# A larger share of the gate table on GpSimd, scalar-form subtractions beside it, and a re-ordered start

## The chip, the cores and the metric

One core of one Trainium2 chip runs the whole program. The metric is device microseconds of one execution; lower is better. Engines are named as the profile names them: PE (TensorE), ACT (ScalarE), DVE (VectorE), POOL (GpSimd), SP (SyncE, which here only issues DMAs).

## The reference, cut to what matters

A decoder trunk of two layers, 256 tokens, width 1024, float32. `c_act = silu(c)`, and per layer `mod = c_act @ w_mod[i] + b_mod[i]` gives six vectors of 1024: shift, scale and gate of the mixer, shift, scale and gate of the expert part. Layer 0 mixes with a gated short convolution (`conv_in`, `conv_out`), layer 1 with multi-scale pooling (`pool_in`, `pool_group`, `pool_out`). Then both do this:

```python
h = modulate(rmsnorm(x, norm2_g[i]), sh2, sc2)
# peer_ffn: 8 heads, product keys 128 x 128 = 16384 experts, 16 chosen per head and token
idx  = e1 * N_KEYS + e2                      # chosen experts of a token
gate = softmax(sc)                           # their weights
act  = gelu(sum_d(xc * u_tab[idx]))
out  = sum(gate * act * v_tab[idx])
x = x + g2 * out
```

A final RMS norm gives the output.

## The kernel before, in words

**The expert part is done densely.** For all 16384 experts, as 128 tiles of 128 experts, PE multiplies the `up` tile with all 256 tokens; ACT applies GELU; the result, `acts` (A), has 128 blocks of 128 experts x 256 tokens. It is then multiplied by a gate matrix that is zero but for the chosen experts, and PE multiplies it with the 128 `down` tiles (`down_banks`, L1779). The `down` tiles are taken in two halves of 64 (half 0, then half 1). Float32 products are made of three products of rounded parts: each weight tile is loaded by SP into `raw` (ring of 4), ACT rounds it to `high` (L546), DVE subtracts to get `low` (`rest_of`, called through `slot`, L833), always three tiles ahead of PE; the moving side is split alike into `mov_h` (ACT L752) and `mov_l` (`low_weight`, DVE L1382).

**The gate matrix comes in three ways.** Tokens 0 to 127: POOL adds the gates into a table in device memory with 128 indirect DMAs per layer (`add_gates`, L494), SP fetches it back, and DVE multiplies it in (`weigh_first`, L1239), two tiles of experts at a time. Tokens 128 to 255, first 64 tiles: DVE builds one-hot matrices of 8 tokens, a "set" (`hots`, L1215, L1217, L1221), PE turns each set into a gate block with 24 matmuls (`scatter`, L1729), DVE multiplies it in (`weigh`, L1233), 16 sets. Same tokens, last 64 tiles: the first `LATE_T` = 80 of them again by POOL (`add_late`, L505: per layer `LATE_S` x 8 heads x 2 = 5 x 8 x 2 = 80 indirect DMAs; then `fetch_late`, L517, and on DVE `weigh_late`, L1247), the other 48 tokens by 6 sets, taken in pairs (48 matmuls) among the first `down` tiles of half 0.

**Order on POOL.** All of `add_gates`; then, once SP has fetched the packed lists of indices and gates (`fetched`, L426; that fetch waits until the sets whose space it overwrites have been built, and stands after `up` tile `LATE_UP` in SP's queue), all of `add_late`; then a wait for all of them to land; then `fetch_late`, four buffers.

**Order on DVE in half 0.** For each of the 64 tiles: `slot`, `low_weight`, `weigh_first`, at some tiles `two_sets`, and at the last three tiles `weigh_late` for the first buffers. DVE takes its instructions in order, so a `weigh_late` whose buffer has not landed holds everything behind it, the next `low` and `mov_l` among them.

**The start.** Sixteen blocks of 512 KB of `w_mod` (scale: m = 1, shift: m = 0, k = 0 to 7) are loaded in ten DMAs (`HEAD`, six of them of two blocks), DVE accumulates them (L856, L857), PE sums over the partitions (L1500), ACT adds the shift (L599), and PE starts the convolution's first two tiles (`first_two`, L1571).

Of the kernel before, what the change touches and what calls it, by code (L numbers as in the profile page):

```python
# [34 lines left out]
LATE_T = 80  # L35
LATE_UP = 112
# [31 lines left out]
HEAD = [(1, 0, 1), (1, 1, 1), (1, 2, 2), (1, 4, 2), (1, 6, 2), (0, 0, 2), (0, 2, 2), (0, 4, 2), (0, 6, 1), (0, 7, 1)]  # L68
# [32 lines left out]
def program(nc, small, x_in, k_t, w_mod, conv_in, conv_out, query, up, down, pool_in, pool_group, pool_out,  # L101
# [8 lines left out]
    with ExitStack() as ctx:  # L110
# [146 lines left out]
        macc_done = sem("macc_done")  # L257
        msum_done = sem("msum_done")
# [57 lines left out]
        def _(sp):  # L316
# [19 lines left out]

            for n, (m, k, ks) in enumerate(HEAD):
# [4 lines left out]
                sp.dma_start(mhead[:, m, k:k + ks],  # L342
                             w_mod[0, k * P:(k + ks) * P, m * D:(m + 1) * D].rearrange("(k p) n -> p k n", p=P)
                             ).then_inc(mhead_in[n], 16)
# [194 lines left out]
        def _(act):  # L539
# [36 lines left out]
            def norm(k):  # L576


                if k == 0:
                    act.wait_ge(x_in_s, 16)  # L580
                    for c in range(DC):
                        square(c)
                elif k % 2:
                    act.dma_start(x_spill, flat2(X)).then_inc(spilled, 16)
                act.wait_ge(stat_done, k + 1)
                nc.scalar.activation(sd, gp[:, 0, 0:TC], ACT.Sqrt, bias=eps[:, 0:1],
                                     scale=1.0 / D).then_inc(sd_done, 1)
                if k == 4:
                    return
                if k == 0:  # L590
                    for n in range(AHEAD):
                        arrived(1, n)
                        nc.scalar.activation(flat(high[n]), tile_row(n), ACT.Copy).then_inc(high_ready, 1)
                shift = mod[:, (3 * (k % 2)) * DC:(3 * (k % 2) + 1) * DC]

                act.wait_ge(mod_taken, 4 * (2, 4, 6, 6)[k])
                for c in range(DC):
                    act.wait_ge(xr_done, DC * k + c + 1)
                    nc.scalar.activation(mov_h[:, c], xr[:, c], ACT.Identity,  # L599
                                         bias=shift[:, c:c + 1]).then_inc(mh_done, 1)  # L600

# [219 lines left out]
        def _(dve):  # L821
# [6 lines left out]
            def rest_of(n):  # L828
# [7 lines left out]
            def slot(n):  # L836

                rest_of(n + AHEAD)
# [20 lines left out]
            def head_mod(m):  # L859

                for n, (block_, k0, ks) in enumerate(HEAD):
                    if block_ == m:
                        dve.wait_ge(mhead_in[n], 16)
                        for k in range(k0, k0 + ks):
                            link(add_mod(m, mhead[:, m, k], k, k == 0))
                dve.sem_inc(macc_done, 1)
# [3 lines left out]
            def finish_mod(layer, m0, m1):  # L870

                sums[0] += 1
                dve.wait_ge(msum_done, sums[0])
# [18 lines left out]
            def norm(k, shift_last=None):  # L892
# [3 lines left out]
                if k == 0:  # L896
                    head_mod(1)
# [8 lines left out]
                if k == 0:  # L906
                    head_mod(0)
                    link(nc.vector.memset(vp[:, :, 0:TAPS - 1], 0.0))
                    finish_mod(0, 1, 2)
# [24 lines left out]
                for c in range(DC):  # L934
                    if k == 0 and c == 2:
                        rest_of(0)
                        shift_last()
                    scaled(c)
                if k == 0:
                    rest_of(1)  # L940
                if k == 2:
                    rest_of(AT[1, "pool_in"] + 2)
                if k < 4:
                    for c in range(DC):
                        rest(c)
                if k == 0:
                    rest_of(2)

# [286 lines left out]
            def weigh_first(layer, q):  # L1235
# [30 lines left out]
            for layer in range(LAYERS):  # L1266
                if layer == 0:
                    norm(0, lambda: finish_mod(0, 0, 1))
# [109 lines left out]
                def low_weight(g):  # L1378
                    if g < KEYS:
                        s = g % RING  # L1380
                        dve.wait_ge(wh_ready, g + (layer * KEYS + 1))
                        nc.vector.tensor_tensor(mov_l[:, s], A[:, g * T:(g + 1) * T], mov_h[:, s].bitcast(F32),  # L1382
                                                ALU.subtract).then_inc(wl_ready, 1)
# [8 lines left out]
                for j in range(FIRST_SET, KEYS):  # L1392
# [6 lines left out]
                    slot(n0 + j)  # L1399
# [91 lines left out]
        def _(pe):  # L1491
# [5 lines left out]
            def mod_products(m, c0=0, c1=DC):  # L1497

                for c in range(c0, c1):
                    ins = nc.tensor.matmul(gp[:, 1, m * DC + c:m * DC + c + 1], macc[:, m, c * P:(c + 1) * P],  # L1500
                                           ones[:, 0:1], start=True, stop=True)
                return ins

            def sum_mod(m):

                if sums[0]:

                    pe.wait_ge(mod_taken, 4 * sums[0])
                sums[0] += 1
                mod_products(m).then_inc(msum_done, 1)  # L1510
# [53 lines left out]
            def first_two(layer, name, evac, evac0):  # L1564

                late = name == "conv_in"
                pe.wait_ge(low_ready, AT[layer, name] + (1 if late else 2))
# [5 lines left out]
                for c in range(DC):  # L1573
                    pe.wait_ge(mh_done, moved[0] * DC + c + 1)
                    for s in range(2):
                        one(s, high, mov_h, c, c == 0, False)
                        if s == 0 or not late:
                            one(s, low, mov_h, c, False, False)
                if late:
                    pe.wait_ge(low_ready, AT[layer, name] + 2)  # L1580
                    for c in range(DC):
                        one(1, low, mov_h, c, False, False)
# [72 lines left out]
            for layer in range(LAYERS):  # L1655
                out_act = layer * (16 + KEYS)
                if layer == 0:
                    square_sums(0, 0, DC)
                    pe.wait_ge(macc_done, 1)
                    sum_mod(1)  # L1660
# [242 lines left out]
```

## Time and profile before

| | us |
|---|---|
| three runs | 1806.35, 1812.38, 1812.19 (median 1812.19) |
| the profiled execution's own time | 1807.06 |
| its span, first to last instruction | 1805.4 |
| PE busy | 1765.9 (98% of the span) |
| DVE busy | 1443.1 (80%) |
| POOL busy | 839.8 (47%) |
| mean granted TensorE clock | 0.992 |

The profile's times are from the span's start. PE is busy nearly throughout, so a change counts as far as it shortens PE's work or makes PE wait. Rows of a timeline give start, duration, engine, source line and operation, and in brackets the engine's idle time before and what ended it.

### The profile page before, as it was taken

To read this page: it belongs to the slowest core of one execution; us is meant where nothing else is said; L and a number is where in the kernel's file an instruction comes from. 1 tells how busy PE (TensorE), PEld (TensorE's weight loads), DVE (VectorE), ACT (ScalarE), POOL (GpSimd) and SP (SyncE) were. 2 spreads that over 40 slices of the span, in tenths; PEclk is the share of its full clock that TensorE was granted. 3 is DMA by queue.
4 is the path that set the end of the run, shared out by engine and by line. 5 is a ranking of instruction groups with operands and counts; after the bars stand their busy time and mean duration, and the time that the engine had idled before them with its cause. 6 is when DMAs were issued, how large, how long until landed. Compare 5 with 4: busy or idle time off the path is not lost.

```text
span 1805.4 us, 34572 instructions
## 1 busy us (share of the span) xinstructions
PE 1765.9 (98%) x11751; PEld 1593.7 (88%) x11751; DVE 1443.1 (80%) x2758; ACT 928.3 (51%) x1449; POOL 839.8 (47%) x489
## 2 busy tenths in 40 slices
PE   6999999999999999999998999999999999999998
PEld 6988999999888888888888899999988888888887
DVE  8998789997777966698888778999787796666665
ACT  3345555555555445454555546556555554545453
POOL 1000066777877888510000005677777888841000
PEclk9999999999999999999999999999999999999998
DMA  8998889867766988999945756777777698886662
GB/s 322 325 338 315 273 256 303 252 175 189 175 172 166 249 233 242 295 362 334 325 164 179 265 164 164 186 179 183 186 175 179 164 244 234 241 262 205 209 207 85
DMA packets 191697, 414.23 MB, mean 229 GB/s; under 512 B 77696, under 2 KB 95488, under 8 KB 190976
## 3 DMA queue, kind: packets, MB, share of 16 engines
q1 hardware_dynamic: 126768, 405.36, 66.7%
q0 software_dynamic: 62976, 5.49, 8.6%
q10 hardware_dynamic: 1872, 2.39, 0.4%
q8 instruction: 40, 0.66, 0.1%
q14 instruction: 41, 0.34, 0.1%
HBM read 387.60 MB, written 25.54 MB: 229 GB/s over the span
## 4 chain that ended last, share of the span: by engine, by line
PE 93%; DVE 5%; issue 1%; DMA 1%; ACT 1%; SPq 0%; DVEq 0%; ACTq 0%
PE acc L1779 38%; PE ps L1597 31%; PE ps L1614 7%; PE acc L1614 5%; PE ps L1617 4%; PE acc L1617 2%; PE gp L1729 2%; DVE acts L857 2%; PE ps L1571 1%; DVE low L833 1%; PE gp L1718 1%; DMA acts<-w_mod 1%; DVE acts L924 0%; PE gp L1533 0%; DVE mov L956 0%
## 5 line engine op out<-in xcount | busy, mean ns | idle before, releaser
L833 DVE TENSOR_TENSOR low<-raw,high 128x1024 fp32r<-128x1024 f32 x596 | 724.0, 1217 | 276.1 <-ACT high L546 273.5
L546 ACT ACTIVATE high<-raw 128x1024 fp32r<-128x1024 f32 (+1 forms) x593 | 624.7, 1054 | 375.3 <-PE acc L1779 300.8
L494 POOL DMA_INDIRECT table<-added x256 | 466.3, 1821 | 585.4 <-DVE added L1080 452.7
L1779 PE MATMUL acc<-high,mov 128*128 128x512 f32 x2048 | 633.9, 390 | 2.7 <-DVE mov L1382 2.7
L1597 PE MATMUL ps<-mov,high 128*128 128x256 f32 x3280 | 594.0, 284 | 7.2 <-issue 2.7
L1597 PEld LDWEIGHTS ps<-mov,high 128*128 128x128 f32 x3280 | 511.0, 192 | 9.1 <-issue 6.1
L1597 PE MATMUL ps<-mov,low 128*128 128x256 f32 x1640 | 463.9, 283 | 0.0
L1779 PEld LDWEIGHTS acc<-high,mov 128*128 128x128 f32 x2048 | 384.4, 188 | 84.4 <-DVE mov L1382 2.7
L1779 PE MATMUL acc<-low,mov 128*128 128x512 f32 x1024 | 398.4, 389 | 0.0
L1597 PEld LDWEIGHTS ps<-mov,low 128*128 128x128 f32 x1640 | 314.6, 192 | 0.0
L1779 PEld LDWEIGHTS acc<-low,mov 128*128 128x128 f32 x1024 | 192.2, 188 | 39.6
L505 POOL DMA_INDIRECT late<-gate x96 | 198.4, 2066 | 35.7 <-issue 28.7
L517 POOL DMA_DIRECT2D mov<-late x64 | 34.7, 544 | 270.2 <-DVE acts L1247 262.2
L691 ACT ACTIVATE acts<-ps 128x256 f32<-128x256 f32 x160 | 61.2, 382 | 191.8 <-PE ps L1597 191.6
L1614 PE MATMUL ps<-mov,high 128*128 128x512 f32 x592 | 149.3, 394 | 0.5 <-DVE low L833 0.5
L505 POOL DMA_INDIRECT late<-idx x64 | 135.6, 2119 | 19.5 <-issue 19.5
L1614 PEld LDWEIGHTS ps<-mov,high 128*128 128x128 f32 x592 | 106.3, 189 | 20.2 <-issue 0.9
L857 DVE SCALAR_TENSOR_TENSOR acts<-acts,cact 128x1024 f32<-128x1024 f32 x86 | 109.9, 1278 | 3.3 <-DMA acts<-w_mod 2.9
L752 ACT ACTIVATE mov<-acts 128x256 fp32r (+1 forms) x256 | 101.9, 400 | 20.0 <-DVE acts L1239 20.0
L1382 DVE TENSOR_TENSOR mov<-acts,mov 128x256 fp32r<-128x256 f32 x256 | 106.5, 418 | 2.3 <-ACT mov L752 2.3
L1614 PE MATMUL acc<-mov,high 128*128 128x512 f32 x384 | 97.0, 394 | 0.0
L1617 PEld LDWEIGHTS ps<-mov,low 128*128 128x128 f32 x592 | 80.8, 190 | 5.8
(156 smaller groups left out, 1410.8 us busy)
## 6 DMA issues: line engine op xcount, KB each, us to landing
raw<-up SPq DMA_DIRECT2D x256, 512.0 KB
raw<-down SPq DMA_DIRECT2D x256, 512.0 KB
acts<-w_mod SPq DMA_DIRECT2D x84, 512.0 KB, 5.8
raw<-query SPq DMA_DIRECT2D x32, 512.0 KB
table<-hot SPq DMA_DIRECT2D x32, 512.0 KB, 6.7
raw<-conv_in SPq DMA_DIRECT2D x24, 512.0 KB
mov<-table SPq DMA_DIRECT2D x96, 128.0 KB, 4.3
acts<-w_mod SPq DMA_DIRECT2D x6, 1024.0 KB, 14.9
```

The source lines that it names most:

```text
L494: nc.gpsimd.indirect_dma_start(table[layer], bass.IndirectOffsetOnAxis(ap=DEST[:, col:col + 1], axis=0), GT0[:, col:col + 1], None, comput ...
L505: nc.gpsimd.indirect_dma_start(table2[layer], bass.IndirectOffsetOnAxis(ap=LATE_AT[m][:, col:col + 1], axis=0), LATE_GATE[m][:, col:col + ...
L546: nc.scalar.activation(taken_of(n, flat(high[s])), taken_of(n, tile_row(s)), ACT.Copy).then_inc(high_ready, 1)
L691: nc.scalar.activation(A[:, bass.ds(i * (RING * T) + (first + s) * T, T)], ps[:, s % 2, 0:T], ACT.Gelu).then_inc(evac_act, 1)
L752: nc.scalar.activation(mov_h[:, s], A[:, bass.ds(g * T, T)] if not isinstance(g, int) else A[:, g * T:(g + 1) * T], ACT.Copy).then_inc(wh_ ...
L833: nc.vector.tensor_tensor(taken_of(n, flat(low[n % RING])), taken_of(n, tile_row(n % RING)), w, ALU.subtract).then_inc(low_ready, 1)
L857: return nc.vector.scalar_tensor_tensor(macc[:, m], tile, c, macc[:, m], ALU.mult, ALU.add)
L1382: nc.vector.tensor_tensor(mov_l[:, s], A[:, g * T:(g + 1) * T], mov_h[:, s].bitcast(F32), ALU.subtract).then_inc(wl_ready, 1)
L1597: ins = nc.tensor.matmul(dst, w[s][:, c], m[:, mv], start=(first and n == 0), stop=(last and n == 2), skip_group_check=skip)
L1614: nc.tensor.matmul(b, high[s][:, c], flat(mov[:, c]), start=(c == 0), stop=(c == DC - 1), skip_group_check=True)
L1617: ins = nc.tensor.matmul(b[:, 0:T], low[s][:, c], mov_h[:, c], start=False, stop=(c == DC - 1), skip_group_check=True)
L1779: ins = nc.tensor.matmul(acc[:, b, :], w[:, s, tok], flat(v[s])[:, cols], start=(opening and n == 0), stop=(closing and n == 2), skip_grou ...
```

## The change

`LATE_T` goes from 80 to 96: `LATE_S` becomes 6, so POOL gets 6 x 8 x 2 = 96 indirect DMAs of `add_late` per layer instead of 80, and four sets remain instead of six. `LATE_UP` goes from 112 to 116. In the `up` tiles from the 81st on and in half 0 of `down`, DVE's subtractions (`slot`, in half 0 also `low_weight`) and the products of `weigh_first` are written as `scalar_tensor_tensor` with a factor 1.0 in place of `tensor_tensor`. At the start every block of `w_mod` has a DMA of its own, DVE does four shift blocks before it finishes the scale and four behind it (the last in two halves), the shift is summed in two halves, and PE takes the high parts of the first two tiles before their low parts, with one filler matmul (`keep_warm`) per chunk.

```diff
-LATE_T = 80
-LATE_UP = 112
+LATE_T = 96
+LATE_UP = 116
-HEAD = [(1, 0, 1), (1, 1, 1), (1, 2, 2), (1, 4, 2), (1, 6, 2), (0, 0, 2), (0, 2, 2), (0, 4, 2), (0, 6, 1), (0, 7, 1)]
+HEAD = [(m, k) for m in (1, 0) for k in range(DC)]
...
+            def two(out, a, b, op, beside_pool=False):
+
+                if beside_pool:
+                    return nc.vector.scalar_tensor_tensor(out, a, 1.0, b, ALU.mult, op)
+                return nc.vector.tensor_tensor(out, a, b, op)
...
-                    nc.vector.tensor_tensor(taken_of(n, flat(low[n % RING])), taken_of(n, tile_row(n % RING)),
-                                            w, ALU.subtract).then_inc(low_ready, 1)
+                    two(taken_of(n, flat(low[n % RING])), taken_of(n, tile_row(n % RING)), w, ALU.subtract,
+                        beside_pool).then_inc(low_ready, 1)
...
+            def finish_shift(c0, c1):
+
+                dve.wait_ge(shift_half, c0 // (DC // 2) + 1)
+                nc.vector.tensor_tensor(mod[:, c0:c1], acc[:, c0 // (DC // 2), c0:c1],
+                                        sm[:, C_BM + c0:C_BM + c1], ALU.add).then_inc(mod_taken, 2)
...
                 if k == 0:
+                    for n in range(4, DC - 1):
+                        link(head_block(0, n))
+                    for h in range(2):
+                        head_block(0, DC - 1, h * D // 2, (h + 1) * D // 2).then_inc(macc_done, 1)
+                    scaled(0)
+                    scaled(1)
+                    finish_shift(0, DC // 2)
+                    scaled(2)
+                    scaled(3)
+                    finish_shift(DC // 2, DC)
+                    sums[0] += 1
+                    scaled(4)
+                    scaled(5)
+                    rest_of(0)
+                    scaled(6)
+                    scaled(7)
                     rest_of(1)
...
-                nc.vector.tensor_tensor(a, a, wt[q % WRING].rearrange("p (g t) -> p g t", t=P),
-                                        ALU.mult).then_inc(weighed, 1)
+                two(a, a, wt[q % WRING].rearrange("p (g t) -> p g t", t=P), ALU.mult, beside_pool
+                    ).then_inc(weighed, 1)
...
-                    slot(n0 + j)
+                    slot(n0 + j, True)
                     fold(side(j - FIRST_SET), j * T).then_inc(folded, 1)
...
-                    slot(n0 + j)
+                    slot(n0 + j, True)
                     if j + AHEAD < HALF:
-                        low_weight(j + AHEAD)
+                        low_weight(j + AHEAD, True)
                     if j < 7:
                         if j % 2 == 0:
-                            weigh_first(layer, j // 2 + 2)
+                            weigh_first(layer, j // 2 + 2, True)
                     else:
-                        weigh_first(layer, j - 1)
+                        weigh_first(layer, j - 1, True)
...
-                    keep_warm(80)
-                    pe.wait_ge(macc_done, 2)
-                    sum_mod(0)
-                    keep_warm(20)
+                    keep_warm(76)
+                    for h in range(2):
+                        pe.wait_ge(macc_done, 2 + h)
+                        sum_shift(h * DC // 2, (h + 1) * DC // 2)
+                    sums[0] += 1
+                    keep_warm(6)
```

## Rows read from the trace of the kernel before

**Rows 1.** The page's chain of waits, shares of the span by line.

```profile
PE acc L1779 38%; PE ps L1597 31%; PE ps L1614 7%; PE acc L1614 5%; PE ps L1617 4%; PE acc L1617 2%; PE gp L1729 2%; DVE acts L857 2%; PE ps L1571 1%; DVE low L833 1%; PE gp L1718 1%; DMA acts<-w_mod 1%; DVE acts L924 0%; PE gp L1533 0%; DVE mov L956 0%
```

**Rows 2.** The chain of waits in order of time: start us, us, what.

```profile
440.07 1.47 PE gp L1729 x48
...
458.38 1.47 PE gp L1729 x48
```

**Rows 3.** POOL's timeline, layer 0, from `add_late` on.

```profile
551.83 2.54 POOL L505 DMA_INDIRECT late<-gate  x1 [4.44 <-DMA table<-added]
...
740.29 2.41 POOL L505 DMA_INDIRECT late<-idx  x1 [0.30 <-issue]
746.77 2.26 POOL L517 DMA_DIRECT2D mov<-late  x4 [4.07 <-DMA late<-idx]
```

**Rows 4.** DVE's timeline, layer 0: the first `weigh_late`.

```profile
751.06 0.32 DVE L1247 TENSOR_TENSOR acts<-acts,mov 128x160 f32<-128x160 f32 x1 [0.94 <-DMA mov<-late]
```

**Rows 5.** The same places of layer 1, POOL's timeline and then DVE's.

```profile
1403.68 2.06 POOL L505 DMA_INDIRECT late<-gate  x1 [2.60 <-DMA table<-added]
...
1592.51 2.43 POOL L505 DMA_INDIRECT late<-idx  x1 [0.30 <-issue]
1598.84 2.26 POOL L517 DMA_DIRECT2D mov<-late  x4 [3.90 <-DMA late<-idx]
...
1610.14 0.32 DVE L1247 TENSOR_TENSOR acts<-acts,mov 128x160 f32<-128x160 f32 x1
```

**Rows 6.** DVE's timeline, then POOL's, in the same microseconds of half 0.

```profile
644.86 1.23 DVE L833 TENSOR_TENSOR low<-raw,high 128x1024 fp32r<-128x1024 f32 x1 [0.82 <-ACT high L546]
646.00 0.42 DVE L1382 TENSOR_TENSOR mov<-acts,mov 128x256 fp32r<-128x256 f32 x1
...
645.09 2.41 POOL L505 DMA_INDIRECT late<-gate  x1 [0.30 <-issue]
```

**Rows 7.** POOL's timeline at another phase against DVE, and DVE's beside it.

```profile
601.51 1.55 POOL L505 DMA_INDIRECT late<-gate  x1 [0.30 <-issue]
603.36 1.55 POOL L505 DMA_INDIRECT late<-gate  x1 [0.30 <-issue]
...
599.71 0.42 DVE L1239 TENSOR_TENSOR acts<-acts,mov 128x256 f32<-128x256 f32 x1
...
603.37 0.46 DVE L1239 TENSOR_TENSOR acts<-acts,mov 128x256 f32<-128x256 f32 x1
```

**Rows 8.** POOL's and DVE's timeline: a scalar-form instruction, in layer 0 and layer 1.

```profile
434.36 1.55 POOL L494 DMA_INDIRECT table<-added  x1 [0.30 <-issue]
...
434.36 0.32 DVE L1194 SCALAR_TENSOR_TENSOR acts<-acts 80x128 f32<-80x128 f32 x1
...
1294.74 0.28 DVE L1194 SCALAR_TENSOR_TENSOR acts<-acts 80x128 f32<-80x128 f32 x1
```

**Rows 9.** Groups by line, shapes kept apart: count, busy us, mean ns, idle before.

```profile
L833 DVE TENSOR_TENSOR low<-raw,high 128x1024 fp32r<-128x1024 f32 x592 | 721.5, 1221 | 276.1 <-ACT high L546 273.5 <-DVE acts L1197 0.2
...
L857 DVE SCALAR_TENSOR_TENSOR acts<-acts,cact 128x1024 f32<-128x1024 f32 x86 | 109.9, 1278 | 3.3 <-DMA acts<-w_mod 2.9
L1382 DVE TENSOR_TENSOR mov<-acts,mov 128x256 fp32r<-128x256 f32 x256 | 106.5, 418 | 2.3 <-ACT mov L752 2.3
...
L930 DVE SCALAR_TENSOR_TENSOR mov<-acts,mod,mov 128x256 fp32r<-128x256 f32 x32 | 13.0, 478 | 0.0
```

**Rows 10.** SP's own queue: the fetch of the packed lists.

```profile
508.29 1.28 SPq L426 DMA_DIRECT2D gate<-shelf  x3
```

**Rows 11.** Busy time by stretch (PE, PEld, DVE, ACT, POOL), granted clock, DMA share, GB/s.

```profile
132.00:139.00 7.00, 4.63 (x36) 4.14 (x34) 6.97 (x10) 2.46 (x5) 0.00 (x0) 1.00 1.00 352
139.00:146.00 7.00, 6.17 (x39) 5.69 (x40) 4.88 (x17) 2.33 (x6) 0.00 (x0) 0.51 0.71 277
```

**Rows 12.** The chain of waits at the start: start us, us, what.

```profile
2.88 9.88 DMA acts<-w_mod
...
46.17 43.44 PE ps L1597 x360
```

More of the change, by code:

```diff
@@ L589, in norm, with first_tile @@
                     return
+                def first_tile(n):
+                    arrived(1, n)
+                    nc.scalar.activation(flat(high[n]), tile_row(n), ACT.Copy).then_inc(high_ready, 1)
                 if k == 0:
-                    for n in range(AHEAD):
-                        arrived(1, n)
-                        nc.scalar.activation(flat(high[n]), tile_row(n), ACT.Copy).then_inc(high_ready, 1)
+                    for n in range(2):
+                        first_tile(n)
                 shift = mod[:, (3 * (k % 2)) * DC:(3 * (k % 2) + 1) * DC]
-                act.wait_ge(mod_taken, 4 * (2, 4, 6, 6)[k])
+                act.wait_ge(mod_taken, 6 if k == 0 else 4 * (2, 4, 6, 6)[k])
                 for c in range(DC):
+                    if k == 0 and c == DC // 2:
+                        act.wait_ge(mod_taken, 8)
                     act.wait_ge(xr_done, DC * k + c + 1)
@@ L906, in norm @@
                 if k == 0:
-                    head_mod(0)
-                    link(nc.vector.memset(vp[:, :, 0:TAPS - 1], 0.0))
+                    for n in range(4):
+                        link(head_block(0, n))
                     finish_mod(0, 1, 2)
@@ L932, in rest @@
                                                    ALU.subtract).then_inc(ml_done, 1)
[L934 to L938, printed above, removed]
-                if k == 0:
+                if k == 0:
+                    for n in range(4, DC - 1):
+                        link(head_block(0, n))
+                    for h in range(2):
[12 more added lines that the diff above has]
+                    scaled(7)
                     rest_of(1)
-                if k == 2:
-                    rest_of(AT[1, "pool_in"] + 2)
-                if k < 4:
+                    dve.wait_ge(mod_taken, 8)
                     for c in range(DC):
                         rest(c)
-                if k == 0:
+                    link(nc.vector.memset(vp[:, :, 0:TAPS - 1], 0.0))
                     rest_of(2)
+                else:
+                    for c in range(DC):
+                        scaled(c)
+                    if k == 2:
+                        rest_of(AT[1, "pool_in"] + 2)
+                    if k < 4:
+                        for c in range(DC):
+                            rest(c)
             moved = [0]
@@ L1381, in low_weight @@
                         dve.wait_ge(wh_ready, g + (layer * KEYS + 1))
[L1382 to L1383 removed]
+                        two(mov_l[:, s], A[:, g * T:(g + 1) * T], mov_h[:, s].bitcast(F32), ALU.subtract,
+                            beside_pool).then_inc(wl_ready, 1)
                 n0 = AT[layer, "up"]
@@ L1571, in one @@
                     return nc.tensor.matmul(ps[:, s, 0:T], w[s][:, c], m[:, c], start=first, stop=last)
-                for c in range(DC):
-                    pe.wait_ge(mh_done, moved[0] * DC + c + 1)
+                if late:
+                    pe.wait_ge(high_ready, 2)
+                    for c in range(DC):
+                        pe.wait_ge(mh_done, moved[0] * DC + c + 1)
+                        for s in range(2):
+                            one(s, high, mov_h, c, c == 0, False)
+                        keep_warm(1)
                     for s in range(2):
-                        one(s, high, mov_h, c, c == 0, False)
-                        if s == 0 or not late:
+                        pe.wait_ge(low_ready, s + 1)
+                        for c in range(DC):
                             one(s, low, mov_h, c, False, False)
-                if late:
+                else:
                     pe.wait_ge(low_ready, AT[layer, name] + 2)
                     for c in range(DC):
-                        one(1, low, mov_h, c, False, False)
+                        pe.wait_ge(mh_done, moved[0] * DC + c + 1)
+                        for s in range(2):
+                            one(s, high, mov_h, c, c == 0, False)
+                            one(s, low, mov_h, c, False, False)
                 lag = DC // 2
```

61 lines of the change are left out of this document (32 added, 29 removed).

## The prediction

> **What bounds the kernel now.** The page's chain of waits is read first, since it says whose work the time is made of: by line it is PE's products and nearly nothing else, with 2% in the one-hot products of L1729 [rows 1]. The one place where a neighbour of PE is nearly late shows in two timelines laid side by side, POOL's and DVE's around tile 61 of half 0. In layer 0 the last `add_late` starts at 740.29 and takes 2.41, so it ends at 742.70; 4.07 later all have landed and the first `fetch_late` is issued at 746.77 [rows 3]. DVE starts the first `weigh_late` at 751.06 after 0.94 us idle for just this buffer [rows 4]. So POOL's chain in layer 0 has no slack at all: it is 0.94 us late. In layer 1 the same step is at 1598.84 and DVE comes at 1610.14 without waiting; with the 4.29 us from issue to use that layer 0 shows (751.06 - 746.77) the slack there is 1610.14 - 1598.84 - 4.29 = 7.0 us [rows 3 to 5]. The change puts 16 more DMAs in front of this point. Whether POOL can take them is the question; all the rest is small.
>
> **What POOL waits for.** The timelines of DVE and POOL over the same microseconds show what one `add_late` costs. The short ones take 1.55 and with 0.30 of issue follow each other by 1.85 [rows 7]. In the steady part of half 0 each takes 2.41 + 0.30 = 2.71, about the 2.72 us of a `down` tile. There POOL starts at 645.09, DVE's L833 has run since 644.86 and gives way to L1382 at 646.00, and POOL ends at 645.09 + 2.41 = 647.50, which is 1.50 after that [rows 6]. So POOL stands still until the `tensor_tensor` with two inputs in SBUF is over, and the next one meets the next tile's L833 in the same way. The reverse is seen too: where POOL and a DVE instruction start together (603.36 and 603.37), POOL is not delayed and DVE's L1239 takes 0.46 in place of 0.42 [rows 7].
>
> **The change, part by part.**
>
> *Fewer sets.* Two sets fewer per layer are one pair of 48 matmuls, 1.47 us on PE's chain with no gap around it [rows 2]. Two layers: -2.94. DVE is rid of one `two_sets` per layer, which hides behind PE.
>
> *Sixteen more indirect DMAs per layer.* Half 0 cannot end before they have landed. They start at 551.83 in layer 0 [rows 3]. The fetch of the packed lists may hold them back: it was at 508.29 [rows 10], and now waits for set 11 in place of set 9, six `up` tiles on, 458.38 - 440.07 = 18.3 us [rows 2], so about 527 plus its landing; the table's own DMAs still end later. With `LATE_UP` at 116, SP stands at this wait with tile 116 and all behind it in its queue; that load comes about one tile and a half late, and a load is issued some seven tiles ahead of PE by the code's waits, so I cost it at nothing; if the cover is gone, it costs about one tile, 3 us.
>
> *The scalar form.* On DVE it costs 1278 - 1221 = 57 ns for a low part and 478 - 418 = 60 ns for each 256-wide product [rows 9], in half 0 57 + 2 x 60 = 0.18 us per tile. That lies in the 0.82 us that DVE idles before each L833 for ACT [rows 6]. With that cover gone it would be 61 x 2 x 0.18 = 22 us. What it does to POOL the trace does not show on a long instruction. Bounds: at best POOL is never held, and the pitch is 1.85; at worst it is held as before, 2.71. The nearest row is the one scalar-form instruction that starts with a POOL DMA, L1194 in layer 0, both at 434.36: it takes 0.32, where the same instruction alone in layer 1 takes 0.28 [rows 8]. That is the same 0.04 that L1239 loses in the same position [rows 7]. The scalar form thus asks for what POOL has, as `tensor_tensor` does. It still reads two tensors in SBUF. I take the worst case, the full hold. The row has one instance, and shows DVE waiting for POOL and not the reverse, which is why the other end keeps a large chance.
>
> The Trainium skill ("SBUF — State Buffer", section "Who interferes with whom") says that a Vector instruction with two SBUF inputs contends with a GpSimd instruction that reads SBUF, and that the first to issue holds the shared pair for its whole length. By that rule the two forms are alike and the sum is the one made below; the rows on `tensor_tensor` agree (1.50 after the end of L833), for the scalar form no row decides.
>
> *The sum with the hold, layer 0.* 16 x 2.71 = 43.4. The third pair of sets is gone, and behind a pair DVE is so busy that POOL slips into the 1.85 pitch; losing some three such DMAs costs 3 x 0.86 = 2.6, an estimate. If DVE ran on, `add_late` would end at 742.70 - 1.47 + 43.4 + 2.6 = 787.2. DVE comes to the first `weigh_late` at 751.06 - 0.94 - 1.47 = 748.65 and stops. From then POOL is free: (787.2 - 748.65) / 2.71 = 14.2 DMAs are left, at 1.85 they take 26.3, to 774.9. Then 4.07 until they have landed and 4.29 until the buffer is there: 783.3. DVE stands for 34.6 in place of 0.94. Behind this `weigh_late` in DVE's order are the next `mov_l` and `low` parts, and PE has about a tile in hand, as now: PE loses 33.7.
>
> *Layer 1.* The last `add_late` ends at 1592.51 + 2.43 = 1594.94 now; with the same additions at 1639.5. DVE stops at 1610.14 - 1.47 = 1608.7; 11.4 DMAs are left, 21.0 us, to 1629.7; then 3.90 and 4.29: 1637.9. PE loses 29.
>
> *The clock.* Where PE had been idle for 2.4 of 7 us, the granted clock of the next 7 us was 0.51 [rows 11], the lower level, 1.2 GHz. After each long stall I add half of 7 us, 3.5: together 7.
>
> *The start.* DVE waits at first for a DMA of two blocks, which lasts 9.88 in the chain [rows 12]. Single blocks let it begin when the first half has landed, about 1.3 us earlier, the length of one block's L857 [rows 9], since DVE then went from block to block without idling for data. Of this, part is given back: the low parts of tiles 0 and 1 stand behind more `scaled` steps, and the last shift block in two halves costs one more instruction's fixed time. PE's unbroken run now begins at 46.17 [rows 12] and depends on the third low part. Bounds: -1.3, and +1.2 if one low part comes late; I take -0.6.
>
> Sum: -2.94 + 33.7 + 29 + 7 - 0.6 = +66. Against the profiled execution's own 1807.06 that is 1873. Its time is 5 us under the median of the three runs, 1812.19, and 0.7 over the lowest, so a median may come 5 higher; I leave the prediction at 1873.
>
> **The rivals.**
>
> *POOL is freed by the scalar form.* All 96 at 1.85 are 178 us: from 551.83 to 729.4, landed at 733.5, fifteen microseconds ahead of DVE. Then nothing waits and most of the 0.94 us is won back too, 0.7: 1807.06 - 2.94 - 0.6 - 0.7 = 1802.8. This ends on the other side, not slower. For it: the form is another instruction with its own pace (57 ns more), and the hold is only shown for `tensor_tensor`. Against: the 0.04 of L1194. The point from which it decides is a mean pitch of (748.65 - 4.07 - 4.29 - 551.83) / 96 = 1.96 us in layer 0, and (1608.7 - 3.90 - 4.29 - 1403.68) / 96 = 2.05 in layer 1 [rows 5]. By this rival and by a median drawn low a gain over 0.5% is possible, hardly more.
>
> *Partly freed.* Only some are held, and the mean pitch is 2.3: `add_late` ends in layer 0 at 551.83 + 96 x 2.3 = 772.6 if DVE runs on, 24 us behind 748.65. Of these, ten DMAs go at 1.85: 767 and 8.4, so 27 us lost; in layer 1 at 1403.68 + 221 = 1624.5, 7 DMAs left, 13 us and 8.2, 21 us lost. With the clock about 1807 + 27 + 21 + 7 - 4 = 1858. At a pitch near 2.05 the loss is under 10 and the time near 1815.
>
> *The scalar form makes DVE the bound.* The 22 us above. Against it: 0.82 idle in each tile, and 0.18 asked; it would need a burst of sets that DVE no longer catches up with, and there are fewer of these now.
>
> **How the numbers follow.** A difference under 0.5%, 9 us, can't be told from none here: the three runs alone spread over 6. Full hold 0.48 (slower). Freed 0.40, of which 0.29 within 0.5% and 0.11 faster, since 4 us of real gain and the spread must add up. Partly freed 0.09, DVE or the start as a new bound 0.03, slower both, but for 0.02 of them within 0.5%. That is slower 0.58, same 0.31, faster 0.11. The likeliest case has its own range of 1855 to 1888: POOL's lateness off by four DMAs either way in both layers, and the clock's 7 in or out. The range for 8 in 10 must reach over the freed case, down to 1799.
>
> **What would show it.** In the profile after: L1729 has 960 matmuls, and 192 rows of L505. In half 0, past the second pair of sets, the rows of L505 last 2.4 to 2.5 if the hold is there, 1.55 if not; this decides all. If it is there, DVE L1247 waits for the DMA of `late` by about 35 and 29 us and PE L1779 for DVE L1382, and the granted clock falls behind it. If not, the first L517 is issued near 733. The unbroken run of PE at the start should begin near 45.6. The prediction is wrong if the low-part rows in scalar form lie over POOL rows that last 1.55.

## Result, and the profile after

| | before | after |
|---|---|---|
| median of the runs, us | 1811.65 (4 runs, 1806.35 to 1812.38) | 1867.18 (4 runs, 1860.57 to 1868.80) |
| ratio after/before | | 1.029, 95% interval 1.0254 to 1.0326 |
| profiled span, us | 1805.4 | 1866.1 |
| mean granted clock | 0.992 | 0.974 |

The kernel is 2.9% slower. 1873 was forecast, with 1855 to 1888 as the likeliest case's own range.

The page's chain of waits, by engine and by line (L1641 and L1825 are PE's products, before L1597 and L1779):

```profile
PE 54%; POOL 29%; issue 6%; DVE 6%; DMA 4%; ACT 1%; SPq 1%; DVEq 0%; POOLq 0%; ACTq 0%
PE ps L1641 22%; POOL late L505 21%; PE acc L1825 19%; POOL table L494 8%; PE ps L1658 4%; PE ps L1661 2%; PE acc L1658 2%; PE ps L1607 2%; DVE low L839 2%; DMA table<-added 1%; DMA raw<-conv_in 1%; PE acc L1661 1%; PE gp L1764 1%; SPq L343 1%; DMA raw<-up 1%
```

Where it was nearly all PE [rows 1], 29% of the span in this chain is now POOL's, 21% in L505 (`add_late`) and 8% in L494 (`add_gates`). That does not mean that POOL's DMAs cost 21% of the time: the chain crosses over to POOL at the two stalls and then follows POOL back. The cost stands in the view of the waits (total, times, longest):

```profile
DVE acts L1284 <- DMA mov<-late: 64.8, 2, 35.1
PE acc L1825 <- DVE mov L839: 63.9, 4, 33.9
```

DVE waits twice, once in each layer, for the buffer of `late`; PE waits for DVE's `mov_l` behind it. Before, the four waits of PE for it summed to 2.7. POOL's timeline in layer 0, to be laid beside [rows 3] and [rows 6]:

```profile
551.92 2.13 POOL L505 DMA_INDIRECT late<-gate  x1 [4.06 <-DMA table<-added]
...
645.93 2.42 POOL L505 DMA_INDIRECT late<-gate  x1 [0.30 <-issue]
...
746.63 2.42 POOL L505 DMA_INDIRECT late<-gate  x1 [0.30 <-issue]
749.35 1.54 POOL L505 DMA_INDIRECT late<-idx  x1 [0.30 <-issue]
751.20 1.55 POOL L505 DMA_INDIRECT late<-idx  x1 [0.30 <-issue]
...
777.10 1.55 POOL L505 DMA_INDIRECT late<-idx  x1 [0.30 <-issue]
780.70 2.25 POOL L517 DMA_DIRECT2D mov<-late  x4 [2.05 <-DMA late<-idx]
```

And DVE's timeline beside it:

```profile
645.71 1.23 DVE L838 SCALAR_TENSOR_TENSOR low<-raw,high 128x1024 fp32r<-128x1024 f32 x1 [0.83 <-ACT high L546]
646.85 0.42 DVE L838 SCALAR_TENSOR_TENSOR mov<-acts,mov 128x256 fp32r<-128x256 f32 x1
...
747.55 0.42 DVE L838 SCALAR_TENSOR_TENSOR acts<-acts,added 128x256 f32<-128x256 f32 x1
783.04 0.36 DVE L1284 TENSOR_TENSOR acts<-acts,mov 128x192 f32<-128x192 f32 x1 [35.07 <-DMA mov<-late]
...
1671.55 0.36 DVE L1284 TENSOR_TENSOR acts<-acts,mov 128x192 f32<-128x192 f32 x1 [29.75 <-DMA mov<-late]
```

Three things are to be read out of the two. First, the low part is now in the scalar form (L838) and the POOL row over it still lasts 2.42. It ends at 645.93 + 2.42 = 648.35, which is 1.50 after L838 hands over at 646.85, the same 1.50 as behind `tensor_tensor` [rows 6]. Second, POOL's rows turn short, 1.54 or 1.55, in the moment in which DVE stands still: from 749.35 to 777.10 there are 1 + 27.75 / 1.85 = 16 of them. Third, with the last of them and 2.05 of landing the fetch comes at 780.70, and DVE goes on 2.34 later.

### The profile page after: what moved, and what is told of

Same layout as the page of the kernel before. It is cut to its first block, busy times and chain, and to the rows that moved or that the text cites. A ratio compares the mean times of both kernels' runs of the same rounds, so it can differ in the third digit from the quotient of the medians.

```text
span 1866.1 us, 34373 instructions
## 1 busy us (share of the span) xinstructions
PE 1766.0 (95%) x11645; PEld 1593.7 (85%) x11645; DVE 1434.0 (77%) x2744; ACT 928.1 (50%) x1449; POOL 908.9 (49%) x521
## 4 chain that ended last, share of the span: by engine, by line
PE 54%; POOL 29%; issue 6%; DVE 6%; DMA 4%; ACT 1%; SPq 1%; DVEq 0%; POOLq 0%; ACTq 0%
PE ps L1641 22%; POOL late L505 21%; PE acc L1825 19%; POOL table L494 8%; PE ps L1658 4%; PE ps L1661 2%; PE acc L1658 2%; PE ps L1607 2%; DVE low L839 2%; DMA table<-added 1%; DMA raw<-conv_in 1%; PE acc L1661 1%; PE gp L1764 1%; SPq L343 1%; DMA raw<-up 1%
## 5 line engine op out<-in xcount | busy, mean ns | idle before, releaser
L494 POOL DMA_INDIRECT table<-added x256 | 469.9, 1835 | 581.4 <-DVE added L1117 448.5
L1825 PE MATMUL acc<-high,mov 128*128 128x512 f32 x2048 | 636.0, 391 | 63.9 <-DVE mov L839 63.9
L1641 PE MATMUL ps<-mov,high 128*128 128x256 f32 x3280 | 595.1, 284 | 6.2 <-issue 2.7
L839 DVE TENSOR_TENSOR low<-raw,high 128x1024 fp32r<-128x1024 f32 x372 | 450.0, 1214 | 164.7 <-ACT high L546 162.9
L1641 PEld LDWEIGHTS ps<-mov,high 128*128 128x128 f32 x3280 | 512.4, 192 | 7.8 <-issue 6.3
L1825 PEld LDWEIGHTS acc<-high,mov 128*128 128x128 f32 x2048 | 386.4, 189 | 145.6 <-DVE mov L839 63.3
L1641 PE MATMUL ps<-mov,low 128*128 128x256 f32 x1640 | 464.6, 283 | 0.0
L1825 PE MATMUL acc<-low,mov 128*128 128x512 f32 x1024 | 399.9, 391 | 0.0
L838 DVE SCALAR_TENSOR_TENSOR low<-raw,high 128x1024 fp32r<-128x1024 f32 x224 | 274.0, 1223 | 122.9 <-ACT high L546 120.4
L1641 PEld LDWEIGHTS ps<-mov,low 128*128 128x128 f32 x1640 | 315.4, 192 | 0.0
L505 POOL DMA_INDIRECT late<-gate x128 | 267.0, 2086 | 45.9 <-issue 38.4
L1825 PEld LDWEIGHTS acc<-low,mov 128*128 128x128 f32 x1024 | 193.4, 189 | 40.0
L517 POOL DMA_DIRECT2D mov<-late x64 | 34.6, 542 | 256.9 <-DVE acts L1284 230.2
L505 POOL DMA_INDIRECT late<-idx x64 | 132.6, 2071 | 19.5 <-issue 19.5
L870 DVE SCALAR_TENSOR_TENSOR acts<-acts,cact 128x1024 f32<-128x1024 f32 x72 | 91.9, 1277 | 0.0
```

The source lines that it names most:

```text
L494: nc.gpsimd.indirect_dma_start(table[layer], bass.IndirectOffsetOnAxis(ap=DEST[:, col:col + 1], axis=0), GT0[:, col:col + 1], None, comput ...
L505: nc.gpsimd.indirect_dma_start(table2[layer], bass.IndirectOffsetOnAxis(ap=LATE_AT[m][:, col:col + 1], axis=0), LATE_GATE[m][:, col:col + ...
L838: return nc.vector.scalar_tensor_tensor(out, a, 1.0, b, ALU.mult, op)
L839: return nc.vector.tensor_tensor(out, a, b, op)
L870: return nc.vector.scalar_tensor_tensor(macc[:, m], tile, c, macc[:, m], ALU.mult, ALU.add)
L1641: ins = nc.tensor.matmul(dst, w[s][:, c], m[:, mv], start=(first and n == 0), stop=(last and n == 2), skip_group_check=skip)
```

## The experiments

In the expectations A is the theory of the prediction: POOL stands through an instruction of DVE that reads two tensors in SBUF, in either form, and sixteen DMAs held in this way are the loss. Ratios are to the kernel before, run beside each kernel on the same chip. The first four kernels take the change apart.

**The tokens alone** (the kernel before with two constants changed):

```diff
-LATE_T = 80
-LATE_UP = 112
+LATE_T = 96
+LATE_UP = 116
```

> The kernel before with 96 tokens in place of 80 and nothing else of the change. Theory A (every long two-input DVE instruction holds POOL, whatever its form; the scalar form does nothing): the same loss as with the whole change, DVE waits near 35 and 30 us at the first weigh_late of each layer, rows of L505 in half 0 at 2.41, time 1867 plus the 0.9 that the new start gives, about 1868. Rival B (the scalar form does relieve POOL in part, so the change hid some of the damage): longer waits than 35 and 30, time above 1875.

Measured: 1871.19 us (1869.76 to 1873.93), ratio 1.034, interval 1.0299 to 1.0381. The waits are those of the whole change, with `tensor_tensor` throughout:

```profile
DVE acts L1247 <- DMA mov<-late: 66.7, 2, 36.9
PE acc L1779 <- DVE mov L1382: 65.8, 4, 35.7
```

The two constants make the whole loss. Rival B, which asked for more than 1875, falls. One row of L505 lasts 7.74 here (from 591.93), which theory A doesn't foresee; it comes back below.

**The scalar form alone** (`slot`, `low_weight` and `weigh_first` as in the change, 80 tokens, the old start; an excerpt of the edit):

```diff
-                    slot(n0 + j)
+                    slot(n0 + j, True)
...
-                        low_weight(j + AHEAD)
+                        low_weight(j + AHEAD, True)
```

> The kernel before, 80 tokens, with the scalar form alone. Theory A: rows of L505 in half 0 stay at 2.41 and the time within 1 us of before (1807 in a profile), since the immediate scalar costs 4 ns on a low part and nothing on the 256-wide products. Rival B: a shorter mean of L505 and no wait of 0.94 us for the late buffer, about 1 us faster.

Measured: 1812.03 (1804.50 to 1819.57, 12 runs), ratio 1.001, interval 0.9986 to 1.0034. The 96 instances of L505 that carry gates (of 160; shortest, median and longest in ns):

```profile
L505 POOL DMA_INDIRECT late<-gate x96: 1546/2402/7736, 545.0 to 1582.9; - x96
```

The median is 2402 ns, as with `tensor_tensor`; the longest, 7.7 us, is again a single row of its kind. The scalar form frees nothing and costs nothing that can be measured. The rival "POOL is freed" falls on this.

**The start alone** (the change with 80 tokens and `LATE_UP` 112, and without the scalar form):

```diff
-                if beside_pool:
-                    return nc.vector.scalar_tensor_tensor(out, a, 1.0, b, ALU.mult, op)
                 return nc.vector.tensor_tensor(out, a, b, op)
```

> The change with 80 tokens and without the scalar form: the new start alone. The profile after shows the end of the convolution stage 0.86 us earlier (first fall of the granted clock at 138.25 in place of 139.11). Expected 0.9 us faster, not measurable in the times; in the profile a span near 1804.5. Rival: the start's gain is lost later in a stage that waits for DVE, span as before.

Measured: 1808.71 (1803.72 to 1818.39, 12 runs), ratio 0.9979, interval 0.9954 to 1.0004. A gain of the start is not told from none. In the profiled execution (span 1810.6) DVE waited once 6.8 us for the buffer of `late`: one row of L505, at 591.27, lasted 7.74, which is 5.3 more than a held one. So here too POOL is at the edge. Behind the convolution PE's first wait for DVE ends at 139.20 here and at 139.72 in the kernel before, 0.52 earlier (0.37 with the whole change, see below), not the 0.86 that the expectation takes from the fall of the clock.

**The change without its sixteen DMAs** (the four sets stay away; the gates of the last sixteen of the 96 tokens are left out of POOL's table, which stays zero there):

```diff
                 for n in range(LATE_S * HEADS):
+                    if n % LATE_S == LATE_S - 1:
+                        continue
                     for k in range(LATE_K):
                         add_late(layer, n, k)
...
-                for n in range(LATE_S):
+                for n in range(LATE_S - 1):
```

> The changed kernel, but POOL leaves out the sixth part of add_late (16 indirect DMAs per layer), so a sixth of the late gates is missing from the output; the rest is as in the change, two sets fewer and the new start too. Theory A: both waits of DVE for the late buffer vanish or stay under 1 us, no clock loss, and the gains stand alone: 1807.1 - 2.9 - 0.9 = 1803. Rival C (the loss is from the other parts of the change: the larger fetches, the later fetch of the lists, LATE_UP): a wait remains and the time stays above 1815.

Measured: 1814.11 (1801.75 to 1827.65, 12 runs), ratio 1.0009, interval 0.9979 to 1.0039. The loss against the kernel before is gone, so it hangs on the number of DMAs. But the median is 11 us above the expected 1803, and the wait did not vanish. By the time alone rival C, which asked for more than 1815, falls only just; it is the view of the waits that says where the 11 us are:

```profile
DVE acts L1286 <- DMA mov<-late: 14.9, 2, 13.9
```

POOL is late even with 80, by 13.9 in layer 0 and 1.0 in layer 1. From the first `add_late` to the end of the last it takes 203.7 in layer 0 (545.04 to 748.69), where the kernel before took 190.9. Two things make this up. With only two pairs of sets left in half 0, fewer of the 80 DMAs are short (22 under 1.9, where 30 were). And one row, at 591.17, lasts 7.74. The spread of 26 us fits a wait that differs from run to run; no low run was profiled.

**Shorter instructions on DVE.** If POOL waits for the end of the instruction that runs, shorter ones should give it 1.85 or near. The low parts are written in two instructions of 512 columns, or four of 256, where the change had the scalar form, with all 96 tokens:

```diff
-                    return nc.vector.scalar_tensor_tensor(out, a, 1.0, b, ALU.mult, op)
...
+                    pieces = 2 if beside_pool else 1
...
+                    for i in range(pieces):
+                        q = slice(i * width, (i + 1) * width)
+                        ins = nc.vector.tensor_tensor(to[:, q], of[:, q], w[:, q], ALU.subtract)
+                    ins.then_inc(low_ready, 1)
```

> The change (96 tokens, new start) with plain tensor_tensor, and each low part from the 81st up tile on and in half 0 done as two instructions of 512 columns. Theory A (POOL stands until the two-input DVE instruction that is running has ended): shorter instructions hold it shorter. By the rows (one half hands over after 0.60 us, POOL needs 1.81 from there to its next start, a tile is 2.72) three of four DMAs meet no or a short remainder and the mean pitch in the steady part falls from 2.72 to 2.04. 96 DMAs then end near 749 in layer 0; DVE waits some 6 us there and about 0 in layer 1: 1806 to 1812. Rival D (POOL gets in only when DVE idles, or it is DVE's total load that counts): the pitch stays 2.72 or grows with the 0.06 us more of DVE work per tile, waits 35 and 30, 1867 or more.

Measured: 1802.52 (1800.34 to 1808.89, 12 runs), ratio 0.9956, interval 0.9939 to 0.9972. The loss is won back, and the kernel is 0.44% faster than before, with 96 tokens. POOL in the steady part of half 0:

```profile
641.76 2.03 POOL L505 DMA_INDIRECT late<-gate  x1 [0.30 <-issue]
644.10 1.82 POOL L505 DMA_INDIRECT late<-gate  x1 [0.30 <-issue]
646.22 1.55 POOL L505 DMA_INDIRECT late<-gate  x1 [0.30 <-issue]
...
649.94 2.03 POOL L505 DMA_INDIRECT late<-gate  x1 [0.30 <-issue]
```

Four DMAs (the line left out is the fourth, at 648.07) in 649.94 - 641.76 = 8.18 us, which is three tiles of 2.72; before it was one in each tile. No wait was left in layer 0, where 6 us were expected, and 7.1 us in layer 1, where none was. Single rows of L505 lasted 7.0 and 7.9 us. Like the rows of 7.74 above they have no place in theory A.

> The same in four instructions of 256 columns, each handing over after 0.335 us. Theory A: mean pitch 1.94, late DMAs end near 740, no wait in either layer, 1803. Rival D: as above and worse, DVE has 0.2 us more work per tile. Rival E (fixed cost of the smaller DVE instructions takes over): POOL is in time but PE waits for low parts behind each pair of sets, time above 1806.

Measured (`pieces = 4`): 1833.19 (1830.92 to 1836.52, 6 runs), ratio 1.0128, interval 1.0102 to 1.0153. Worse than halves by 31 us, and 1803 was missed. The steady part is as expected, four DMAs from 642.19 to 650.02, 1.96 each; the time is lost in a few rows behind the first pair of sets. POOL:

```profile
586.34 6.07 POOL L505 DMA_INDIRECT late<-idx  x1 [0.31 <-issue]
592.71 18.26 POOL L505 DMA_INDIRECT late<-idx  x1 [0.30 <-issue]
611.27 1.54 POOL L505 DMA_INDIRECT late<-idx  x1 [0.30 <-issue]
```

DVE at the end of the 18.26:

```profile
608.80 0.41 DVE L837 TENSOR_TENSOR mov<-acts,mov 128x256 fp32r<-128x256 f32 x1
609.14 0.41 DVE L837 TENSOR_TENSOR acts<-acts,mov 128x256 f32<-128x256 f32 x1
609.47 1.27 DVE L1273 TENSOR_TENSOR acts<-acts,gp 128x512 f32<-128x512 f32 x2
```

DVE has fallen behind with the sets and runs without a gap, one instruction with two SBUF inputs after the other. POOL passes many of their ends without getting in. It ends at 592.71 + 18.26 = 610.97, and 1.50 before that, at 609.47, DVE begins L1273, whose second input, `gp`, is in PSUM. The row of 6.07 ends in the same way, 1.50 after an L1273 that begins at 590.91. So it isn't enough that an instruction ends. But it isn't always such an instruction that lets POOL in either: layer 1's row of 16.26 (from 1467.77) ends 1.51 after 1482.52, where one two-input instruction hands over to the next and DVE is not idle:

```profile
1482.18 0.41 DVE L837 TENSOR_TENSOR acts<-acts,added 128x256 f32<-128x256 f32 x1
1482.52 1.42 DVE L849 TENSOR_TENSOR low<-raw,high 128x256 fp32r<-128x256 f32 x4
```

The expectations of the door below say of both long rows that an input in PSUM ended them; that holds for the one of 18.26 only.

**Less slack needed, and fewer tokens.** Two kernels ask about the 7.1 us left in halves. The first puts the first three `weigh_late` behind the last tile of half 0:

```diff
-                    if j >= HALF - 3:
-                        weigh_late(layer, j - (HALF - 3))
-                for g in range(AHEAD):
-                    low_weight(HALF + g)
+                weigh_late(layer, 0)
+                low_weight(HALF)
+                low_weight(HALF + 1)
+                weigh_late(layer, 1)
+                low_weight(HALF + 2)
+                weigh_late(layer, 2)
```

> low_in_halves with the first three weigh_late moved from the last three tiles of half 0 to behind its last tile. Theory A: DVE asks for the late buffer some 5 us later, so the 6 us of waiting in layer 0 are nearly covered: 1803 to 1806, at the price of at most about 1 us per layer where PE waits for the first mov_l of half 1.

Measured: 1804.39 (1802.45 to 1809.72, 12 runs), ratio 0.9967, interval 0.9951 to 0.9983. The wait for `late` (in layer 1 again) fell from 7.1 to 3.0, but PE's waits for `mov_l` only from 8.3 to 7.3 in all, since the later place adds 0.6 in layer 0. In the time nothing is gained.

The second has halves with 80 tokens:

```diff
-LATE_T = 96
-LATE_UP = 116
+LATE_T = 80
+LATE_UP = 112
```

> low_in_halves with 80 tokens. Theory A: POOL's chain gets 20 to 25 us of slack in place of none, so the late buffer is never waited for, and if the executions of the kernel before above 1807 come from this wait, the spread of times shrinks too: 1805 to 1807 in all runs. Rival F (the spread has another origin): no wait in the profile, but times still spread from 1804 to 1820.

Measured: 1805.32 (1804.11 to 1808.05, 12 runs), ratio 0.9974, interval 0.9959 to 0.999. The fetch goes out at 707.36, 39 us earlier than in the kernel before and with more slack than the 20 to 25 us expected, nothing waits, and the runs lie within 4 us where the start alone and the form alone spread over 15. That the spread comes from the wait for `late` is supported by this, not shown run by run.

**A door for POOL.** The theory formed on quarters (G in the expectations): in an unbroken train of two-input instructions POOL can miss any number of ends, and one instruction with no such input lets it in. So one `memset` of one column was put on DVE in each tile of half 0, behind `weigh_first`:

```diff
+                    if len(doors) >= DC:
+                        need(doors[-DC])
+                    doors.append(did(nc.vector.memset(ctmp[:, j % DC:j % DC + 1], 0.0)))
```

> low_in_quarters with one memset of one column on DVE per tile of half 0, behind weigh_first: 62 ns that read no tensor. In low_in_quarters one L505 lasted 18.26 us (592.71 on) and one of layer 1 16.3 us, both while DVE ran two-input instructions back to back; POOL went on where a product with an input in PSUM began. Theory G (between two-input instructions that follow without a gap POOL may fail to get in, and any instruction that reads at most one SBUF tensor lets it in): no L505 longer than about 3.5 us in half 0, the late DMAs end some 20 us earlier than 752.5, no wait for the late buffer, 1803. Rival H (it is DVE's lack of idle time, a full queue, that shuts POOL out): the long rows remain, and with 0.06 us more of DVE work per tile the time is 1833 or more.

Measured: 1803.93 (1803.20 to 1814.73, 12 runs), ratio 0.9985, interval 0.9967 to 1.0004, against 1.0128 without the `memset`. In the same stretch, behind the first pair of sets, POOL's rows are

```profile
587.97 1.72 POOL L505 DMA_INDIRECT late<-idx  x1 [0.30 <-issue]
...
591.85 2.20 POOL L505 DMA_INDIRECT late<-idx  x1 [0.30 <-issue]
...
596.20 1.70 POOL L505 DMA_INDIRECT late<-gate  x1 [0.30 <-issue]
598.21 1.73 POOL L505 DMA_INDIRECT late<-gate  x1 [0.30 <-issue]
```

and the door itself, on DVE, with the rows that the text below names, is

```profile
592.55 0.41 DVE L1255 TENSOR_TENSOR hot<-sm,idx 128x512 bf16<-128x512 bf16 x1
...
596.42 0.41 DVE L849 TENSOR_TENSOR low<-raw,high 128x256 fp32r<-128x256 f32 x1
596.43 0.06 DVE L1471 MEMSET ctmp<- 128x1 f32 x1
...
598.12 0.06 DVE L1471 MEMSET ctmp<- 128x1 f32 x1
598.44 1.08 DVE L849 TENSOR_TENSOR low<-raw,high 128x256 fp32r<-128x256 f32 x3
```

An instruction of 0.06 us takes away rows of 18.26 and 16.26: the longest row of L505 in half 0 is now 2.20, in either layer (rows of up to 4.53 stand before it, in the `up` stage, where there is no `memset`). Rival H falls. That the `memset` itself is what lets POOL in, as theory G has it, these rows do not show. The DMA of 596.20 ends 1.47 after the first `memset`, but one two-input instruction hands over to the next in the same moment. The DMA of 598.21 ends at 599.94, 1.82 after the second `memset` and 1.50 after an ordinary hand-over at 598.44. And the DMA of 591.85 got in at 592.55, also at an ordinary hand-over, 3 us after the last `memset`. The edit also brings a semaphore wait and shifts DVE by a little in each tile; an instruction as short with two inputs in SBUF, in the same place, was not tried.

> The same memset in low_in_halves, whose longest L505 were 7.0 us in layer 0 and 7.9 in layer 1, in the same place. Theory G: none above 3.5 us, the wait of 7.1 us in the profile of low_in_halves gone, median 1800 to 1802 with a narrower spread than 1800 to 1809. Rival H: unchanged, 1802.5 with the same spread.

Measured (the same lines in halves): 1801.84 (1798.99 to 1806.32, 12 runs), ratio 0.9956, interval 0.9936 to 0.9976, span 1800.0. No wait for `late` is left, and the longest row of L505 in half 0 is 2.07, where halves alone had 7.0 and 7.9. POOL's last rows in layer 0:

```profile
728.90 1.81 POOL L505 DMA_INDIRECT late<-idx  x1 [0.30 <-DMA late<-idx]
734.96 2.25 POOL L517 DMA_DIRECT2D mov<-late  x4 [4.26 <-DMA late<-idx]
```

DVE takes that buffer at 746.53, 11.6 us after the issue. By the ratio it is no better than halves alone, 0.9956 for both; these two are the best versions, 0.44% under the kernel before.

## Why the prediction was right, and where its terms were off

**What POOL waits for.** Right, and it carried the forecast. The scalar form holds POOL as `tensor_tensor` does: 2.42 against 2.41, and 1.50 after the hand-over. The form alone has the ratio 1.001, and the sixteen DMAs with their sets 1.034. The nearest row, the 0.04 that L1194 lost beside a POOL DMA [rows 8], pointed the right way on one instance.

**The sum.** DVE's stalls were forecast as 34.6 and 29.2 (1637.9 - 1608.7), and measured 35.07 and 29.75. PE's waits rose from 2.7 to 63.9, 61.2 more, where 62.7 were in the sum. Two terms inside were off and cancelled. The drain was taken as 4.07 and 3.90; it was 2.05 and, in layer 1, 2.22. The way from issue to use was taken as 4.29 from the kernel before, and was 2.34 and 2.31. In layer 0 that is 4.0 too much. Against it sixteen short DMAs were left when DVE stood, not 14.2: 1.8 more at 1.85, 3.3 us (in layer 1 thirteen, not 11.4). The term behind this is the short rows lost with the third pair of sets: three were estimated, and of the 30 rows under 1.9 in layer 0 only 23 were left outside the stall, seven fewer; in layer 1 22 of 29. So the close hit on the stalls, 34.6 against 35.07, is in part luck. The fetch of the lists and `LATE_UP` were costed at nothing, rightly: the lists are fetched at 526.30 (527 was forecast), and `add_late` starts at 551.92, where it was 551.83.

**The clock.** The windows of after, with PE's, PEld's, DVE's, ACT's and POOL's busy time and then the granted clock:

```profile
745.00:752.00 7.00, 7.00 (x32) 5.79 (x32) 2.14 (x4) 3.18 (x3) 6.08 (x4) 1.00 0.92 264
...
759.00:766.00 7.00, 0.00 (x0) 0.00 (x0) 0.00 (x0) 0.00 (x0) 5.79 (x4) 0.50 0.49 99
787.00:794.00 7.00, 6.74 (x23) 5.42 (x24) 4.72 (x9) 1.37 (x2) 1.08 (x2) 0.75 0.67 214
794.00:801.00 7.00, 7.00 (x33) 5.79 (x32) 7.00 (x10) 3.75 (x6) 0.54 (x1) 1.00 0.81 287
...
1674.00:1681.00 7.00, 5.22 (x12) 4.14 (x13) 4.47 (x10) 1.44 (x3) 1.61 (x3) 0.50 0.84 253
1681.00:1688.00 7.00, 7.00 (x31) 5.76 (x30) 3.44 (x6) 3.87 (x6) 0.27 (x1) 0.98 0.36 108
```

The clock falls to 0.50, the level of 1.2 GHz, while PE stands, and comes back some 3 us after PE goes on at 787.26; in layer 1 it stays low through the 5.22 us that PE works up to 1681. The loss is 0.25 x 6.7 = 1.7 us in the first window and half of 5.22, 2.6, in the other: together 4.3 where 7 were in the sum. A term of the right kind, mis-sized.

**The scalar form's own cost.** The groups of after, by form:

```profile
L839 DVE TENSOR_TENSOR low<-raw,high 128x1024 fp32r<-128x1024 f32 x368 | 447.4, 1219 | 164.7 <-ACT high L546 162.9
L838 DVE SCALAR_TENSOR_TENSOR low<-raw,high 128x1024 fp32r<-128x1024 f32 x224 | 274.0, 1223 | 122.9 <-ACT high L546 120.4 <-issue 2.3
L839 DVE TENSOR_TENSOR mov<-acts,mov 128x256 fp32r<-128x256 f32 x134 | 55.5, 418 | 2.3 <-ACT mov L759 2.3
L838 DVE SCALAR_TENSOR_TENSOR mov<-acts,mov 128x256 fp32r<-128x256 f32 x122 | 51.1, 418 | 0.0
L870 DVE SCALAR_TENSOR_TENSOR acts<-acts,cact 128x1024 f32<-128x1024 f32 x72 | 91.9, 1277 | 0.0
```

57 ns were predicted for a low part and 60 for a 256-wide product; they cost 4 and 0. The rows from which the price was taken [rows 9] have a scalar that is read from a column of a tensor (L870 here, still 1277); with the constant 1.0 the form costs next to nothing. No run changed the scalar alone, so that it makes the difference is a reading. It lay in idle time, so the time did not notice. The rival in which DVE becomes the bound rested on this price, and falls with it.

**The sets and the start.** PE has 960 matmuls of the one-hot products, as forecast, -2.94. The start gains less than the -0.6 that was taken: behind the convolution PE's first wait for DVE ends at 139.35, where it ended at 139.72, 0.37 earlier. DVE begins its unbroken run of six blocks early:

```profile
11.44 7.89 DVE L878 SCALAR_TENSOR_TENSOR acts<-acts,cact 128x1024 f32<-128x1024 f32 x6 [2.37 <-DMA acts<-w_mod]
```

PE's unbroken run starts at 43.21 in place of 46.17 [rows 12], where 45.6 was forecast. But most of this isn't kept. The clock that PE was granted from 32 to 39 is 0.55, where it was 1.00, and the end of the convolution hangs on DVE's blocks, which are themselves only 0.36 earlier (L870 at 136.74, L857 at 137.10 before). In all: -2.94 + 61.2 + 4.3 - 0.4 = 62.2, and the spans differ by 1866.1 - 1805.4 = 60.7; 1.5 stay unexplained.

**The rivals.** "POOL is freed" and "partly freed" both fell with the form alone. The point at which the case turns was put at a mean pitch of 1.96 us in layer 0 and 2.05 in layer 1. Layer 1 bears it out: halves come to 2.12 there (1398.32 to 1602.16), and 96 x 0.07 is the 7 us of the wait. In layer 0 they come to 2.08 and don't wait, because `add_late` starts at 537.9 in this trace, 14 us earlier than the 551.83 of the forecast. With the door nothing waits.

**What stays open.** In the steady part POOL gets in when one two-input instruction hands over to the next (the 1.50 behind L833 and L838), and in the train behind the sets it may not for 18 us. What decides between the two is not shown. The position against DVE's instructions does not, as far as the traces resolve it. Here are the same two places in after and in the start alone:

```profile
591.17 0.68 DVE L1254 TENSOR_TENSOR hot<-sm,idx 128x1024 bf16<-128x1024 bf16 x1
591.49 1.78 POOL L505 DMA_INDIRECT late<-gate  x1 [0.30 <-issue]
...
590.95 0.68 DVE L1252 TENSOR_TENSOR hot<-sm,idx 128x1024 bf16<-128x1024 bf16 x1
591.27 7.74 POOL L505 DMA_INDIRECT late<-gate  x1 [0.30 <-issue]
```

Both DMAs start 0.32 after the same instruction of the same train. One gets in at the next hand-over, the other 6 us later, where DVE leaves a small gap (an instruction of 0.41 from 597.17, the next at 597.66). The traces of the form alone, the tokens alone and the kernel without its sixteen DMAs have this row of 7.74 too, those of before and after do not. So with 1024 columns as well a train can shut POOL out. Whether the same kernel has the row in some executions and not in others, which would also spread its times, can't be seen from one trace each.

## What to carry to other kernels

Before work is added to an engine off the chain, work out its slack to the one instruction that others queue behind: here 80 DMAs fitted with none to spare, and sixteen more at 2.71 us cost 60 us. Here the engine slowed by a neighbour's instruction was helped by making that instruction shorter, not by writing the same reads in another form. Shorter pieces also lengthened the waits in a gapless train, from 7.74 to 18.26, so look at the longest row, not the median alone.

## What the runs showed of the hardware

- An indirect DMA of GpSimd takes 1.55 us while VectorE stands still. In the steady part, beside a VectorE instruction that reads two tensors in SBUF, it ends 1.50 us after that instruction hands over, the same for `tensor_tensor` and `scalar_tensor_tensor` (medians of 2402 ns in both kernels).
- The Trainium skill ("SBUF — State Buffer", section "Who interferes with whom") says that a VectorE instruction with two SBUF inputs contends with a GpSimd instruction that reads SBUF, and that the port pair they share is an exclusive lock. This case agrees for single instructions, in both forms. For a back-to-back train it is more than that: the wait went over many instructions, up to 18.26 us. It ended where VectorE began one with an input in PSUM (18.26, 6.07), at a small gap (7.74) or at an ordinary hand-over (16.26). One `memset` of 0.06 us in each tile, with its semaphore wait, took 29 us off the kernel (1833.19 to 1803.93; as a ratio 1.0128 to 0.9985); how it does so stays open.
- `scalar_tensor_tensor` with a constant costs 1223 ns for 1024 columns, `tensor_tensor` 1219; with a scalar read from a tensor it costs 1277.
- After PE had stood for 33.9 us the granted clock stayed at its lower level for about 3 us of work, after 28.6 us for about 5.
